# Gates stage: three buffers for the split weights, four row buffers, two one-hot tiles

## The reference, cut to what matters

```python
q = (h @ w_q)...; s = jnp.einsum('bthcd,hckd->bthck', q, keys)
s_top, i_top = lax.top_k(s, 16)            # for both halves of the key
cand = s_top[..., 0, :, None] + s_top[..., 1, None, :]
best_s, pos = lax.top_k(cand, 16); gates = softmax(best_s)
pre = jnp.einsum('ced,cd->ce', jnp.take(u_tab, ii, axis=0), hh)
out = jnp.einsum('ce,ced->cd', gelu(pre) * gates, jnp.take(v_tab, ii, axis=0))
```

## Time and profile before

| what | value |
|---|---|
| median of the runs | 4571.91 us |
| the profiled execution | 4570.1 us, span 4568.4 us |
| PE busy | 4062.0 us (89%) |
| DVE, ACT, POOL busy | 3121.7, 1898.0, 1492.6 us |
| transfers | 1025.96 MB, mean 225 GB/s |
| gates stage, layer 0: first to last Gelu | 746.9 to 1615.6 us |
| gates stage, layer 1: first to last Gelu | 3286.0 to 3968.4 us |

### The profile page before, as it was taken

The page is one execution under the profiler, slowest core; times in us unless marked ns, Lnnn a source line. Parts: engine busy times, 40 slices in busy tenths (PEclk is TensorE's granted clock), DMA queues, the critical chain, the costliest instruction groups (busy, mean ns, idle before and its releaser), DMA issues. The chain is left out here.

```text
span 4568.4 us, 62858 instructions
## 1 busy us (share of the span) xinstructions
PE 4062.0 (89%) x20380; PEld 3461.7 (76%) x20380; DVE 3121.7 (68%) x5714; ACT 1898.0 (42%) x3664; POOL 1492.6 (33%) x1048
## 2 busy tenths in 40 slices
PE   8687697899999989999978889867799999899998
PEld 2576586778888868888856767645699999899997
DVE  0675378998887668888874454534887765477777
ACT  1211222577777722222223333322257777533332
POOL 0122123555554434444412111102354444322221
PEclk9798898999999999999998898878899999899999
DMA  6333113799999999999941010011278888799996
GB/s 249 130 139 110 41 43 107 244 326 324 330 329 327 343 345 375 373 375 372 374 165 60 33 37 28 28 37 65 75 246 294 282 275 292 261 333 331 336 330 221
DMA packets 411875, 1025.96 MB, mean 225 GB/s; under 512 B 33968, under 2 KB 182448, under 8 KB 405680
## 3 DMA queue, kind: packets, MB, share of 16 engines
q1 hardware_dynamic: 301104, 621.00, 38.7%
q0 software_dynamic: 110592, 402.70, 24.6%
HBM read 904.03 MB, written 119.54 MB: 224 GB/s over the span
## 5 line engine op out<-in xcount | busy, mean ns | idle before, releaser
L156 PE MATMUL psum<-h_hi,w_hi 128*128 128x512 f32 (+1 forms) x2880 | 1140.1, 396 | 309.9 <-POOL w_lo L133 294.5
L129 ACT ACTIVATE w_hi<-w_raw 128x1024 fp32r<-128x1024 f32 x624 | 660.5, 1059 | 1471.1 <-PE psum L1215 863.0
L133 POOL TENSOR_TENSOR w_lo<-w_raw,w_hi 128x1024 fp32r<-128x1024 f32 x258 | 640.7, 2484 | 1471.2 <-ACT w_hi L129 1469.1
L157 PE MATMUL psum<-h_lo,w_hi 128*128 128x512 f32 (+1 forms) x2880 | 1095.4, 380 | 0.0
L158 PE MATMUL psum<-h_hi,w_lo 128*128 128x512 f32 (+1 forms) x2880 | 1094.9, 380 | 0.0
L156 PEld LDWEIGHTS psum<-h_hi,w_hi 128*128 128x128 f32 x2880 | 560.5, 195 | 396.1 <-POOL w_lo L133 188.6
L133 DVE TENSOR_TENSOR w_lo<-w_raw,w_hi 128x1024 fp32r<-128x1024 f32 x366 | 448.4, 1225 | 537.4 <-ACT w_hi L129 513.0
L1213 PE MATMUL psum<-a_hie,w_hi 128*128 128x512 f32 (+1 forms) x2048 | 758.9, 371 | 34.5 <-DVE a_loe L1266 34.5
L1214 PE MATMUL psum<-a_loe,w_hi 128*128 128x512 f32 (+1 forms) x2048 | 756.9, 370 | 0.0
L1215 PE MATMUL psum<-a_hie,w_lo 128*128 128x512 f32 (+1 forms) x2048 | 749.2, 366 | 0.0
L1198 POOL DMA_INDIRECT v_rowse<-in_peer_v,expert_idx x384 | 423.6, 1103 | 825.9 <-DVE row_sume L1275 812.8
(11 more groups left out here) (200 smaller groups left out, 4437.9 us busy)
## 6 DMA issues: line engine op xcount, KB each, us to landing
w_raw<-in_peer_u SPq DMA_DIRECT2D x256, 512.0 KB
w_raw<-in_peer_v SPq DMA_DIRECT2D x256, 512.0 KB
gates<-stageg SPq DMA_DIRECT2D x28, 2048.0 KB
acts<-act_gg SPq DMA_DIRECT2D x128, 256.0 KB
gte<-gates SPq DMA_DIRECT2D x32, 1024.0 KB
act_fe<-acts SPq DMA_DIRECT2D x128, 256.0 KB
ada_w<-in_ada_w SPq DMA_DIRECT2D x12, 2048.0 KB, 7.7
ada_rows<-in_ada_w SPq DMA_DIRECT2D x48, 512.0 KB, 3.5
```

The lines of the kernel that those rows point to most:

```text
L129: act.activation(self.w_hi[:, s, :], self.raw[:, slot, :], ACT.Copy).then_inc(self.hi_done, 1)
L133: pool.tensor_tensor(self.w_lo[:, s, :], self.raw[:, slot, :], self.w_hi[:, s, :].bitcast(F32), ALU.subtract).then_inc(self.lo_done, 1)
L156: pe.matmul(out, wh, hi[:, k], start=(k == 0), stop=False)
L157: pe.matmul(out, wh, lo[:, k], start=False, stop=False)
```

## The change

A third buffer is added for the high and the low part of the weights, in this stage alone (`t.more`, `weights`, W = 3). `hi` of tile c+3 now waits for the product of tile c, where `hi` of tile c+2 did. DVE's `lo` for an even tile stands at step 8(c-2), 8 steps sooner than before. To make room, the row buffers go from 5 to 4 and the 0/1 tiles from 3 to 2. POOL asks, beside tile c, for rows up to `dots_by((c - 3) * KC) + UBUF`, where it was `dots_by(c * KC) + UBUF`. RAW stays 4, and SP's part isn't touched.

```diff
-UBUF = 5
+UBUF = 4
     def hi(self, act, i, slot, s, turn):
         act.wait_ge(self.raw_in[slot], turn * 16 + (self.raw_at[slot] + 16))
-        act.wait_ge(self.tile_done, i + (self.tiles + 1))
-        act.activation(self.w_hi[:, s, :], self.raw[:, slot, :], ACT.Copy).then_inc(self.hi_done, 1)
+        act.wait_ge(self.tile_done, i + (self.tiles + 1 - len(self.more)))
+        act.activation(self.weights(s)[0], self.raw[:, slot, :], ACT.Copy).then_inc(self.hi_done, 1)
...
-    EQ, OJ = 3, 2
+    EQ, OJ, W = 2, 2, SPLIT + 1
...
+        t.more = [(sb("w_hi", [P, D], F32R)[:], sb("w_lo", [P, D], F32R)[:])]
...
                         if p % KC == 0:
-                            low(p // KC + 1)
+                            low(p // KC + 2)
...
                     t.wait_product(act, c)
-                    if c + SPLIT < NKEYS:
-                        t.hi(act, c + SPLIT, (c + SPLIT) % RAW, c % SPLIT, (c + SPLIT) // RAW)
+                    if c + W < NKEYS:
+                        t.hi(act, c + W, (c + W) % RAW, c % W, (c + W) // RAW)
...
-                for i in range(SPLIT):
+                for i in range(W):
                     t.hi(act, i, i, i, 0)
...
-                        t.lo(pool, c, c % RAW, c % SPLIT)
-                    upto = dots if c == NKEYS - 1 else dots_by(c * KC) + UBUF
+                        t.lo(pool, c, c % RAW, c % W)
+                    upto = dots if c == NKEYS - 1 else dots_by((c - 3) * KC) + UBUF
```

More of the change, by code:

```diff
@@ L98, in __init__ @@
         self.wide = 2
+        self.more = []
     def sem(self, name):
@@ L119, in settle, with weights @@
         eng.sem_inc(self.settled, 1)
+    def weights(self, x):
+        if x < SPLIT:
+            return self.w_hi[:, x, :], self.w_lo[:, x, :]
+        return self.more[x - SPLIT]
     def load(self, sp, src, i, slot, n_raw, turn):
@@ L127, in hi @@
         act.wait_ge(self.raw_in[slot], turn * 16 + (self.raw_at[slot] + 16))
-        act.wait_ge(self.tile_done, i + (self.tiles + 1))
-        act.activation(self.w_hi[:, s, :], self.raw[:, slot, :], ACT.Copy).then_inc(self.hi_done, 1)
+        act.wait_ge(self.tile_done, i + (self.tiles + 1 - len(self.more)))
+        act.activation(self.weights(s)[0], self.raw[:, slot, :], ACT.Copy).then_inc(self.hi_done, 1)
     def lo(self, pool, i, slot, s):
         pool.wait_ge(self.hi_done, i + (self.tiles + 1))
-        pool.tensor_tensor(self.w_lo[:, s, :], self.raw[:, slot, :], self.w_hi[:, s, :].bitcast(F32),
-                           ALU.subtract).then_inc(self.lo_done, 1)
+        hi, lo = self.weights(s)
+        pool.tensor_tensor(lo, self.raw[:, slot, :], hi.bitcast(F32), ALU.subtract).then_inc(self.lo_done, 1)
     def context_h(self, scope, tag):
@@ L144, in moving, with product @@
         return x + ([(self.hc_hi[:], self.hc_lo[:])] if tokens == TOK else [])
-    def product(self, pe, i, s, moving, ks=range(KC)):
+    def product(self, pe, i, s, moving, ks=range(KC), w=None):
         if ks[0] == 0:
@@ L151, in product @@
         for k in ks:
-            wh = self.w_hi[:, s, k * P:(k + 1) * P]
-            wl = self.w_lo[:, s, k * P:(k + 1) * P]
+            wh, wl = (x[:, k * P:(k + 1) * P] for x in self.weights(s if w is None else w))
             for n, (hi, lo) in enumerate(moving):
@@ L852, in low @@
                         dve.wait_ge(t.lo_done, c + (t.tiles + RAW))
-                        t.lo(dve, c, c % RAW, c % SPLIT)
+                        t.lo(dve, c, c % RAW, c % W)
                 def dots_to(upto):
@@ L948, in select @@
                     return sparse
+                low(0)
+                low(1)
                 for n, (end, sparse, b) in enumerate(order):
@@ L1005, in _ @@
                             group(group_at[p])
-                        t.product(pe, c, c % SPLIT, moving, [k])
+                        t.product(pe, c, c % SPLIT, moving, [k], c % W)
             @block.scalar
@@ L1127, in _ @@
                     sp.wait_ge(stored[x], 16 * (n // 2 + 1))
-        t.wide = 2
+        t.wide, t.more = 2, []
         t.count_rows(dots, UBUF)
```

## The result

The changed kernel takes 4978.75 us (median of 4 runs, 4972.8 to 4994.84) beside 4570.98 us for the kernel before (4566.15 to 4576.68): a ratio of 1.0897, with a 95% interval of 1.0868 to 1.0926. The forecast was 5026 us, in a range of 4800 to 5220. The profiled execution has a span of 4971.1 us, 402.7 more than before.

A forecast was written before the change was run, and what follows sets the result against it. PE was taken to bound both gates stages before the change. Afterwards two loops would set 8.98 us a dense tile in layer 0 (+225 us) and 7.43 in layer 1 (+231): 456 us on 4570.1, 5026 us, range 4800 to 5220.

The forecast's parts named there:

- PE's waits for `w_lo` go and give nothing: Both gates stages: waits of about 80 us go, but nothing is taken off, as they lie inside the compared tile times.
- The load loop of one tile: Gelu, raw load, `hi`, next Gelu: 2.04 us plus the load in layer 0, 1.94 plus the load in layer 1.
- Its price at a store: At a store of gates, SP issues one load 7 us late, and two loads take 7.4 and 5.6 us.
- The row loop of two tiles, layer 0 only: Layer 0, from `hi` through row request, row, DVE and ACT's scaling to next `hi`: 15.5 us for two tiles.
- The lead of layer 0: Layer 0's 16 lead tiles, paced by the load loop: 2.04 + 4.0 = 6.04 us a tile.
- Small buffers at nothing: Two 0/1 tiles were costed at nothing, DVE being behind PE; some tenths of a us were they level.
- Rows alone: Rival, 0.09: loads mostly land in time; layer 0 grows by 90 us, layer 1 gains some 35; about 4625 us.
- Faster: Rival, 0.04: loads are there, rows just ahead, and the third buffer removes the `w_lo` waits: 4490 us.
- Gain and loss even out: Rival, 0.02: the change's gain and loss cancel, leaving the whole kernel at about 4570 us.
- The clock: Rival, 0.05: PE idles 2 to 3 us in every tile and falls back to 1.2 GHz; about 5500 us.

The follow-up runs named there:

- the row repair: The changed kernel, with POOL asking beside a given tile for the rows of 16 more steps: 4892.7 us, ratio 1.0693 to the kernel before.
- the best kernel reached by another way: The kernel before, with two weight buffers, raw loads issued one tile sooner and rows asked for 8 steps later: 4489.07 us, ratio 0.9806.
- both repairs: The changed kernel, with rows asked for 16 steps further and raw loads issued one tile sooner: 4525.85 us, ratio 0.9901 to the kernel before.

## Why the prediction was right, and where its sizes were off

Both loops were there, in the layers named for them. The stages were to grow by 225 and 231 us and grew by 237.5 and 168.3. The largest error is one term, the price of a store.

**PE's waits for `w_lo` go and give nothing.** Right. They went but for the start of the stage, and the stages grew.

**The load loop of one tile.** Right, and shown: with the loads one tile sooner layer 1 lost its whole growth. The terms of the loop account for the stage. Over all of layer 1's loads, those behind stores among them, I count in the trace 4.45 us on average from issue to landing, and 0.29 us beyond the 0.39 between Gelu and issue, and 112 of 124 `hi` start within 0.3 us of the landing; 1.94 + 4.45 + 0.29 = 6.68 us a tile, and 850.7 / 127 is 6.70.

**Its price at a store.** This term was mis-sized. I let SP issue one load in each round 7 us late, and took 7.4 and 5.6 us for two loads. In layer 1 that lifted a round of nine tiles by 23.9 - 2 x 6.14 = 11.6 us over ordinary ones. Measured in the trace over eleven stores, the tile behind a store takes 10.25 us from Gelu to Gelu and the next one 6.36, where the other dense tiles take 6.41 on average: a round is lifted by 3.8 us. The load behind the store was issued 3.1 us late on average (1.1 to 6.4) and took 5.16 us, the next 4.29. The view above shows a mild case: after the store of gates at 3814.74 the next store of activations took 1.48 us to issue, and the load went out at 3821.47, 1.55 us behind its Gelu (3819.45 to 3819.92) where 0.39 is usual: 1.16 us late. The 7 us came from two rows that were not typical. The 11.2 us between store and load in layer 1 are the longest of that layer's twelve, whose mean is 7.6, and the 15.9 us of layer 0 stand against a mean of 12.5. In the changed kernel the means are 6.9 and 10.0 us, and as its tiles are slower, the Gelu also comes later behind the store, when less of the hold-up is left. The ordinary tile was a little too low in return (6.14 against 6.41), since its load takes 4.47 us and not 4.2. Layer 1 came out at 850.7 us, not 914.

**The row loop of two tiles, layer 0 only.** Right, and shown from three sides: taking it away emptied DVE's waits for rows, leaving it alone kept layer 0 at 1054 us, and it could be made without a third buffer. The pair was put at 15.5 us. Measured between Gelus of the dense part it has a minimum of 15.23, a median of 16.98 and a mean of 17.86 us. The turn shown above says where: 3.72 against 3.71 to the ask, 4.66 against 5.0 for the row, but 5.93 against 4.5 for DVE, whose 2.28 us piece of `select` lay in the way, and 3.62 against 2.34 between scaling and `hi`, as copies of gates and a late load stood there too. That turn's row was a quick one: over the stage's 92 waits for a row it was 5.9 us on average from ask to use, not 5.0. With the store again too dear in return, two errors cancel. The two tiles behind a store take 12.03 and 9.11 us and the others 8.29, so that a round is lifted by 4.6 us, not 8.6, while the others were put at 7.75; 8.98 us a dense tile was predicted, 8.91 measured. The load loop of this layer was put too low as well, at 6.24 us a tile: the loads of those other tiles took 5.49 us, and by itself, with the row repair, it ran at 8.11 us a tile. That layer 0 came within 13 us (1093 against 1106.2) is partly luck.

**The lead of layer 0.** Off: 6.04 us a tile predicted, 7.34 measured, 21 us over its 16 tiles. The loads of its turns (tiles 4 to 19) took 4.76 us on average and not 4.0, which is 0.8 of the 1.3. The other 0.5 lies in three turns. Two were 1.4 us longer, as ACT loaded its tables anew (1.28 us) for the Gelu behind an exponential of `select`. One was 5.8 us longer: there PE stood for 11.0 us for the end of DVE's `select`, and DVE had just waited 16.4 us for a row. With the row repair that wait of PE is gone and the lead took 6.82 us a tile. So the row loop, which I had let begin only behind the lead, already worked in it.

**Small buffers at nothing.** Right within what can be measured, where rows are asked for early; in the changed kernel itself it wasn't tried.

**The rivals.** *Rows alone* is false: it left layer 1 35 us shorter, and that layer grew by 168. *Faster* is false for this kernel, yet its figure, 4490 us for all waits gone, is what the best kernel reached by another way (4489.07). That the two agree is chance: there PE still waits for `w_lo`, and is busy for less. *Gain and loss even out* is false.

**Two slips in the working** change little. 4570.1 + 456 leaves out the 1.8 us to the median, and a row of 3.2 us in place of 5.0 would make the row loop 6.85 us a tile, not 7.1, and the forecast some 70 us shorter, not 50.

**The clock.** PE's granted clock did fall, from 0.98 and 0.97 to 0.90 and 0.91, and by stretches it went lower. Windows of the kernel after, columns as above; the first is the turn of the row loop:

```profile
897.90:915.83 17.93, 16.16 (x66) 13.34 (x67) 14.01 (x18) 12.29 (x28) 7.08 (x6) 0.79 0.69 234
1137.20:1152.90 15.70, 15.19 (x78) 12.56 (x77) 11.23 (x25) 9.07 (x23) 6.17 (x5) 1.00 0.71 234
```

In the first, after waits, twelve matmuls in a row start 0.43 us apart, as at the lower level of 1.2 GHz, and the later ones 0.23. The Trainium skill, TensorE: Matmul & The Clock Gate, section "HAM oscillation", has it that a loop of matmuls that waits for transfers keeps losing its clock. The trace agrees in part: the share fell, and PE was busy 81 us longer in layer 0 for the same matmuls (828.67 to 909.60), but it never stayed down. It was hardly what set the pace: PE stood idle for 196.6 us there, and ACT's `hi`, the start of both loops, waited for PE for 32.5 us where it had been 179.8. With both repairs, which leave the clock alone, the share in the two stages is back at 1.00 and 0.99 and PE busy for 823.84 us in layer 0, so its fall came with the waits. No run holds the clock apart from the waits, so its share in those 32.5 us stays open.

## What to carry to other kernels

A deeper buffer lets a consumer run sooner, and is worth nothing until what feeds the consumer moves by as much; here it was worth nothing even then. Count, in tiles, the distance from the instruction that releases a transfer to the one that waits for it, before and after, on every queue. If the waiting instruction stands ahead of the releasing one on the same engine, that distance of one closes a loop whose period is the transfer's latency and the few instructions around it (4.45 of 6.70 us here), and no engine has to be busy in it. Look behind the name of a wait as well: about half of PE's waits for `w_lo` were late loads, and issuing these sooner won with two buffers what a third was meant to bring.

## What the runs showed that was not expected

SP is held up behind a 2 MB store of gates, and for less time in the slower kernel. The issue of a store of activations in layer 0, kernel before and kernel after (min/median/max in ns):

```profile
L1120 SPq DMA_DIRECT2D acts<-act_gg x128: 332/333/10722, 747.6 to 1616.2; - x128
```

```profile
L1130 SPq DMA_DIRECT2D acts<-act_gg x128: 332/333/4001, 745.2 to 1851.4; - x128
```

The longest hold-up is 4.0 us where it had been 10.7, for two reasons. Counted in the trace over 15 stores, from the issue of the store to the end of the next issue, SP was taken up for 12.5 us on average before, at 307 GB/s, and for 9.9 now, at 241; with both repairs, at 316 GB/s, it is 12.6 again. And the next issue comes later in the slower kernel, 7.4 us behind the store where it was 5.7. That the other traffic sets how long SP is held fits these numbers, but no run changed it alone.

POOL's subtraction for `w_lo` usually takes 2.4 us; beside a 128x2048 piece of DVE's `select` (1208.12, 2.29 us) one took nearly twice that. POOL, layer 0, kernel after:

```profile
1208.14 4.53 POOL L141 TENSOR_TENSOR w_lo<-w_raw,w_hi 128x1024 fp32r<-128x1024 f32 x1 [9.67 <-ACT w_hi L136]
```

It stands in the row loop and lengthens that turn, but few do so: 7 of 72 in the stage took over 3 us (2 before), and the median is 2.40. That DVE's piece is the cause isn't tested.
